# A mixture-of-experts kernel whose expert rows move through device memory, with wider weight blocks and one stream of weight tiles

## The reference, cut to what matters

```python
D_MODEL, N_EXPERTS, TOP_K = 1024, 8, 2
D_FF = 2816

def swiglu(x, wg, wu, wd):
    return jnp.dot(jax.nn.silu(jnp.dot(x, wg)) * jnp.dot(x, wu), wd)

def moe_swiglu(x, router, wg, wu, wd):        # all in float32
    xf = x.reshape(-1, shp[-1])
    logits = jnp.dot(xf, router).astype(jnp.float32)
    top_v, top_i = lax.top_k(logits, TOP_K)
    probs = jax.nn.softmax(top_v, axis=-1)
    gate = jnp.sum(jax.nn.one_hot(top_i, N_EXPERTS, dtype=jnp.float32) * probs[..., None], axis=1)
    y = jnp.zeros(xf.shape, jnp.float32)
    for e in range(N_EXPERTS):
        y = y + gate[:, e:e + 1] * swiglu(xf, wg[e], wu[e], wd[e]).astype(jnp.float32)
    return y
...
x = layer_norm(DEEPNORM_ALPHA * x + moe_swiglu(...), ln_ffn_g[1], ln_ffn_b[1])
```

## Time and profile before

| what | value |
|---|---|
| time, median of 3 runs | 1351.56 us (1350.29 to 1352.23) |
| span of the profiled execution, first to last instruction | 1350.1 us |
| profiled execution's own time | not listed apart; its span is 0.2 to 2.1 us under the three times |
| PE busy | 1262.2 us, 93% |
| DVE busy / ACT busy / POOL busy | 1046.8 / 802.5 / 56.5 us |
| DMA moved | 332.66 MB, mean 246 GB/s |
| mean granted TensorE clock | 0.974 |

### The profile page before, as it was taken

One profiled execution on the slowest core, in us unless ns is written; L12 is line 12 of the kernel. 1 busy time (PEld: TensorE's weight loads), 2 busy tenths in 40 slices (PEclk: granted clock), 3 DMA queues, 4 the chain that ended last, 5 costly groups with the idle time before them and its releaser, 6 DMA issues.

```text
span 1350.1 us, 22286 instructions
## 1 busy us (share of the span) xinstructions
PE 1262.2 (93%) x8696; PEld 1174.4 (87%) x8696; DVE 1046.8 (78%) x1016; ACT 802.5 (59%) x901; POOL 56.5 (4%) x34
## 2 busy tenths in 40 slices
PE   6999999989875989999999999999999999999993
PEld 4899999979874869999998998998998998998992
DVE  6734343469998668889889889888888888888886
ACT  3533333354653456766776766776776776776771
POOL 0000000001642000000000000000000000000000
PEclk9999999999887989999999999999999999999997
DMA  9854444253030407998998998998998998998931
GB/s 276 266 172 157 159 158 150 60 158 105 13 121 32 156 32 237 370 358 284 370 361 277 367 363 278 366 363 275 367 363 279 366 350 292 365 366 282 366 140 37
DMA packets 249538, 332.66 MB, mean 246 GB/s; under 512 B 6404, under 2 KB 222820, under 8 KB 249450
## 3 DMA queue, kind: packets, MB, share of 16 engines
q1 hardware_dynamic: 249283, 331.28, 73.2%
q10 hardware_dynamic: 199, 0.62, 0.2%
HBM read 330.44 MB, written 2.84 MB: 247 GB/s over the span
## 4 chain that ended last, share of the span: by engine, by line
PE 80%; DVE 14%; ACT 3%; issue 2%; DMA 1%; DVEq 0%; ACTq 0%
PE bank L1068 35%; PE bank L1088 18%; PE bank L889 15%; PE bank L918 6%; DVE cacc L1321 5%; PE bank L1032 2%; PE bank L1077 1%; PE bank L838 1%; DVE w_lo L1165 1%; PE bank L1053 1%; ACT w_hi L543 1%; DVE acc L1469 1%; DMA spool<-in_state_pool_dram 1%; PE bank L874 1%; DVE uc_lo L1349 1%
## 5 line engine op out<-in xcount | busy, mean ns | idle before, releaser
L1165 DVE TENSOR_TENSOR w_lo<-raw,w_hi 128x2048 fp32r<-128x2048 f32 x309 | 707.9, 2292 | 200.7 <-ACT w_hi L543 200.1
L543 ACT CAST w_hi<-raw 128x2048 fp32r<-128x2048 f32 x309 | 590.9, 1913 | 260.2 <-PE bank L889 107.6
L1068 PE MATMUL bank<-w_hi,xg_hi 128*128 128x256 f32 x1408 | 401.6, 285 | 5.3 <-DVE acc L1469 3.6
L1068 PE MATMUL bank<-w_hi,xg_lo 128*128 128x256 f32 x1408 | 394.0, 280 | 0.0
L1068 PE MATMUL bank<-w_lo,xg_hi 128*128 128x256 f32 x1408 | 393.9, 280 | 0.0
L1068 PEld LDWEIGHTS bank<-w_hi,xg_hi 128*128 128x128 f32 x1408 | 265.4, 189 | 13.2 <-issue 8.9
L1068 PEld LDWEIGHTS bank<-w_lo,xg_hi 128*128 128x128 f32 x1408 | 266.0, 189 | 3.2
L1068 PEld LDWEIGHTS bank<-w_hi,xg_lo 128*128 128x128 f32 x1408 | 265.2, 188 | 0.0
L889 PE MATMUL bank<-x_hi,w_hi 128*128 128x304 f32 (+1 forms) x544 | 166.2, 305 | 8.5 <-DVE x_lo L1252 5.3
L889 PE MATMUL bank<-x_hi,w_lo 128*128 128x304 f32 (+1 forms) x544 | 164.3, 302 | 0.0
L889 PE MATMUL bank<-x_lo,w_hi 128*128 128x304 f32 (+1 forms) x544 | 163.6, 301 | 0.0
(11 more groups left out here) (191 smaller groups left out, 1337.8 us busy)
## 6 DMA issues: line engine op xcount, KB each, us to landing
raw<-in_moe_w_gate_dram SPq DMA_DIRECT2D x88, 1024.0 KB, 5.6
raw<-in_moe_w_up_dram SPq DMA_DIRECT2D x88, 1024.0 KB, 5.9
raw<-in_moe_w_down_dram SPq DMA_DIRECT2D x88, 1024.0 KB, 5.2
raw<-in_conv_w_dram SPq DMA_DIRECT2D x12, 1024.0 KB, 5.4
raw<-in_ffn_w_gate_dram SPq DMA_DIRECT2D x11, 1024.0 KB, 8.0
raw<-in_ffn_w_up_dram SPq DMA_DIRECT2D x11, 1024.0 KB, 8.1
raw<-in_ffn_w_down_dram SPq DMA_DIRECT2D x11, 1024.0 KB, 4.9
poolw<-in_pool_w_dram SPq DMA_DIRECT2D x1, 1024.0 KB, 11.1
```

Source lines behind the costliest of these rows:

```text
L543: act.copy(w_hi[t % SPLIT][:], raw[t % RAW][:]).then_inc(hi_ready, 1)
L1068: last = pe.matmul(bank[:, 0:TW], x[:, c, :], w[:, c, :], start=(c == 0 and k == 0), stop=(c == KC - 1 and k == 2))
L1165: dve.tensor_tensor(w_lo[t % SPLIT][:], raw[t % RAW][:], w_hi[t % SPLIT][:], ALU.subtract).then_inc(split_ready, 1)
```

## The change

Rows are no longer picked and spread by matmuls. The kernel makes a table `x_dram` in device memory (8 experts x 384 rows of 4 KB) and fills it with zeros from SBUF during the dense gate and up phase: 24 transfers of 0.5 MB on SP's queue, and one for the first 128 rows of `y_dram`. After the router, POOL writes each of the 288 rows to the places of its two experts by 6 indirect DMAs, the offsets `row_i` coming from a few small DVE steps. ACT's queue loads an expert's 128 rows as `xg_rows`, an expert ahead; PE transposes them as before. Each of the first seven experts' outputs is copied to `y_rows` by ACT and stored to `y_dram`. During the last expert POOL fetches each row's two outputs (6 indirect DMAs into freed ring buffers), and DVE adds them to `acc` with weights `w_a` and `w_b` in 6 steps of 128 x 1024. Only the last expert still goes through `sel`, `sel_t` and the 12 scatter matmuls.

Gate and up blocks are 512 columns wide, two tiles each (512 of the 1024 rows, rows of 2 KB); a tile is 12 matmuls of 512 columns. 2816 columns are five such blocks and one of 256. There are still 33 tiles an expert. Their order is g g u u d d, the down tiles being those of the block before. The stream runs on over experts: the next expert's first gate and up tiles stand before the last down tile of this one.

The core of the diff:

```diff
+    BW = 2 * TW
+    NB = (F + BW - 1) // BW
+    def body_tiles(last):
+        tiles = []
+        for j in range(1, NB):
+            for kind in "gu":
+                tiles += [(kind, j, half) for half in range(width(j) // TW)]
+            tiles += [("d", j - 1, half) for half in range(width(j - 1) // TW)]
+        if not last:
+            tiles += [("next " + kind, 0, half) for kind in "gu" for half in range(width(0) // TW)]
+        return tiles + [("d", NB - 1, half) for half in range(width(NB - 1) // TW)]
...
+                if i >= 4 and EMPTY_ROWS // 6 * (i - 4) < EMPTY_ROWS:
+                    for k in range(EMPTY_ROWS // 6 * (i - 4), EMPTY_ROWS // 6 * (i - 3)):
+                        sp.dma_start(x_dram[k * P:(k + 1) * P, :], zero_rows[:]).then_inc(empty, 16)
...
+            pool.wait_ge(empty, 16 * EMPTY_ROWS)
+            pool.wait_ge(rows_known, 1)
+            for i in range(3):
+                pool.wait_ge(x_rows_done, 2 * i + 2)
+                for k in range(2):
+                    pool.indirect_dma_start(x_dram[:, :], bass.IndirectOffsetOnAxis(ap=row_i[0:n, i, k:k + 1], axis=0),
+                                            acc[0:n, i, :], None).then_inc(x_scattered, 16)
+            def one_pass(r):
+                pool.wait_ge(pair_ready, r + 1)
+                pool.wait_ge(split_ready, r * (E * TE) + SPARE_FREE)
+                pool.wait_ge(y_stored, (r + 1) * (16 * (E - 1)) + 16)
+                for k in range(2):
+                    for i in range(3):
+                        pool.indirect_dma_start(y_got[k][i][0:n, :], None, y_dram[:, :],
+                                                bass.IndirectOffsetOnAxis(ap=pair_i[0:n, k, i:i + 1], axis=0))\
+                            .then_inc(y_fetched, 16)
...
+            def load_rows(r, e):
+                act.dma_start(xg_rows[:], x_dram[bass.ds(e * ROWS + r * P, P), :]).then_inc(xg_landed, 16)
...
             def one_expert(r, e, last):                                   # ACT
+                if not last:
+                    load_rows(r, e + 1)
+                for k, (kind, j, half) in enumerate(LAST if last else BODY):
+                    if k + SPLIT < len(tiles) or not last:
+                        hi(t + SPLIT, n)
+                    if kind == "g" and half == width(j) // TW - 1:
+                        turn_evac(n, j - 1)
+                        silu(n, j, t)
...
+                    act.wait_ge(y_stored, (r * (E - 1) + e) * 16 + 16)
+                    for k in range(2):
+                        act.copy(y_rows[:, k * HALF:(k + 1) * HALF], ps[6 + k][:, :]).then_inc(y_out, 1)
+                    act.wait_ge(y_out, 2 * n + 4)
+                    act.dma_start(y_dram[bass.ds(e * P, P), :], y_rows[:]).then_inc(y_stored, 16)
...
+            act.wait_ge(x_scattered, 16 * 6)
+            load_rows(0, 0)
...
-            def gather_rows(g):                                           # PE
...
+            def turn_rows(g):
+                pe.wait_ge(xg_landed, 16 * g + 16)
...
+            def rows_block(n, t, bank, j, half):
+                wh, wl = block_of(w_hi[t % SPLIT], j), block_of(w_lo[t % SPLIT], j)
+                chunks = range(4 * half, 4 * half + 4) if width(j) == 2 * TW else range(KC)
+                for c in chunks:
+                    for k, (x, w) in enumerate(((xg_hi, wh), (xg_hi, wl), (xg_lo, wh))):
+                        last = pe.matmul(bank[:, 0:width(j)], x[:, c, :], w[:, c - chunks[0], :],
+                                         start=(c == 0 and k == 0), stop=(c == KC - 1 and k == 2))
...
+            def add_fetched(r, k, i):                                     # DVE
+                dve.scalar_tensor_tensor(out=acc[0:n, i, :], in0=y_got[k][i][0:n, :], scalar=(w_a, w_b)[k][0:n, i:i + 1],
+                                         in1=acc[0:n, i, :], op0=ALU.mult, op1=ALU.add).then_inc(y_added, 1)
```

More of the change, by code:

```diff
@@ L785, in one_pass @@
+            def one_pass(r):
+                n = r * E
+                xg_evac(n)
+                for p, (kind, j, half) in enumerate(LEAD):
+                    hi(T_MOE + p + SPLIT, n)
+                    if kind == "g" and half == width(0) // TW - 1:
+                        silu(n, 0, T_MOE + p)
                 with act.Fori(0, E - 1) as e:
@@ new lines, in turn_h, with down @@
+            def turn_h(n, j):
+                pe.wait_ge(h_done, n * NB + (FC + j + 1))
+                for s in range(width(j) // P):
+                    last = pe.transpose(ps[4 + j % 2][:, s * P:(s + 1) * P], hn[:, s * P:(s + 1) * P], ident[:])
+                last.then_inc(h_turned, 1)
+            def down(n, t, j, half):
+                pe.wait_ge(split_ready, n * TE + (t + 1))
+                pe.wait_ge(ht_lo_done, n * NB + (j + 1))
+                if j == 0 and half == 0:
+                    pe.wait_ge(y_out, 2 * n + 2)
+                wh, wl = tall(w_hi[t % SPLIT]), tall(w_lo[t % SPLIT])
+                for s in range(TR):
+                    for col in range(2):
+                        cols = slice(col * HALF, (col + 1) * HALF)
+                        for k, (x, w) in enumerate(((ht_hi, wh), (ht_hi, wl), (ht_lo, wh))):
+                            last = pe.matmul(ps[6 + col][:, :], x[:, 2 * half + s, :], w[:, s, cols],
+                                             start=(j == 0 and half == 0 and s == 0 and k == 0),
+                                             stop=(j == NB - 1 and s == TR - 1 and k == 2))
+                last.then_inc(tile_used, 1)
@@ L1457, in _ @@
[L1457 to L1471 removed]
+            one, two = row_of[:, :, 0], row_of[:, :, 1]
@@ new lines, in _ @@
+            (base_a, base_b, slot_a, slot_b, left_a, left_b, gate_a, gate_b, first, other, below, in_a, in_b, at_a,
+             at_b, far_b, w_a, w_b) = (pair[:, i, :] for i in range(18))
+            dve.tensor_tensor(first, one, two, ALU.is_lt)
+            dve.tensor_tensor(other, one, two, ALU.is_gt)
+            dve.tensor_tensor(base_a, top_f[:, :, 0], top_f[:, :, 1], ALU.min)
+            dve.tensor_tensor(base_b, top_f[:, :, 0], top_f[:, :, 1], ALU.max)
+            dve.tensor_tensor(slot_a, one, two, ALU.min)
@@ new lines, in _ @@
+            link(dve.tensor_tensor(slot_b, one, two, ALU.max))
+            dve.tensor_tensor(gate_a, first, prob[:, :, 2], ALU.mult)
+            dve.tensor_tensor(at_a, other, prob[:, :, 3], ALU.mult)
+            dve.tensor_tensor(gate_b, other, prob[:, :, 2], ALU.mult)
+            dve.tensor_tensor(at_b, first, prob[:, :, 3], ALU.mult)
+            dve.tensor_scalar(below, base_b, float(E - 1), None, ALU.is_lt)
+            dve.scalar_tensor_tensor(out=left_a, in0=base_a, scalar=-float(ROWS), in1=slot_a, op0=ALU.mult, op1=ALU.add)
@@ L1473, in xg_low, with select @@
+            def select(e):
+                for i in range(3):
+                    last = dve.tensor_scalar(sel[:, i, :], slot_no[:], slot_of[:, i, e:e + 1], None, ALU.is_equal)
+                last.then_inc(sel_ready, 1)
             def xg_low(g):
```

593 lines of the change are left out of this document (296 added, 297 removed).

## The result

The changed kernel takes 1319.63 us (median of four runs, 1316.71 to 1320.77) against 1350.92 (1349.76 to 1352.23): a ratio of 0.9764, 95% interval 0.975 to 0.9777. The forecast was 1302 with a range of 1292 to 1322; the point is 18 us too low. The profiled execution took 1320.68 us with a span of 1318.8.

The account below looks back on a forecast made before the run. PE was taken to bound the kernel, with DMA near its limit. Span 1350.1, less 62.5 for the stream, plus 10.4 at the start and 2.1 at the end, gave 1300.1, so 1301.6 us (likeliest 1302), range 1292 to 1322.

Parts of the forecast that it names:

- B: Rival at expert borders: ACT's issues or the store's wait cost 2.5 us a border, not 0.5; 1316 us, chance 0.11.
- C: Rival at the start: indirect scatter DMAs take 4.45 us each, start at 530; 1319 us, chance 0.12.
- A: The forecast's own mechanism for the whole kernel: likeliest 1302 us, own range 1293 to 1309, chance 0.66.
- five signs of being right: Expert period near 94.7 us, wide tile 2.75, PE's only DMA wait the first, first weight matmul near 513, end 27.
- A wide tile takes 2.75 us: Expert stream on PE: 12 matmuls of 512 columns cost a down tile's 2.75 us, bounds 2.56 and 2.83.
- At least 1 us is left everywhere: Inside an expert: ACT's and DVE's copies, splits and ht_lo are ready at least 1 us before PE wants them.
- 0.5 us of stall at a border: Between experts: ACT's crowded queue costs nothing to 2 us a border; 0.5 taken, 3.5 for seven.
- DMA: Expert stream: DMA stays just behind PE, 93.4 us an expert against PE's 94.7, needing 364 GB/s.
- D: Rival in the stream: DMA paces it, all bytes held to 348 GB/s; stream 793, time 1335 us, chance 0.04.
- E: Rival in the stream: two DMA queues together drag the rate, slower than before if below 341 GB/s; chance 0.04.
- The start: Router to first weight matmul: six scatters 12 us, row load, transposes and split; 513.1, 10.4 later than before.
- F: Rival: 512 columns bring nothing and new stalls lose half the saving; 1326 us or more, chance 0.03.

Follow-up runs that it names:

- e9: e1 with its small SBUF buffers, stationary operands among them, at the bytes they had in the kernel before, including a 64-byte pad; 1297.8 us, ratio 0.9615.
- e12: e1 with only a pad of 64 bytes, moving every buffer behind the constants and keeping their order; 1299.53 us, ratio 0.962.
- e1: Changed kernel, but at an expert's narrow block ACT evacuates ht_hi and DVE makes ht_lo before the next tile's split; 1307.48 us, ratio 0.9679.
- e4: Changed kernel, but in the mixture DVE computes only the first quarter of each w_lo tile; single run, 1307.9 us.
- e3: Changed kernel, but each expert tile's load moves only 64 KB of its 1 MB; single run, 1315.67 us.
- e7: e1 with each wide tile loaded as 1024 rows of 1 KB instead of 512 of 2 KB; 1307.99 us, ratio 0.9685.
- e5: Changed kernel with blocks of 256 columns and every evacuation, row transposes' too, ahead of the next split; 1327.68 us, ratio 0.9835.
- e11: e1 with ScalarE making only the first quarter of each expert w_hi and VectorE of each w_lo; single run, 1307.45 us.
- e10: e1 plus 54 small filler matmuls while PE waits for the first expert's rows; 1307.52 us, ratio 0.9686.

## Why the forecast was right, and where it was not

The mechanism held in the main: the removed gather, scatter and `sel` work leaves the stream, the ring keeps up, and the start pays part of it back. That the time lies inside the range is in part luck. The forecast gave its own mechanism 1293 to 1309, and 1319.6 is outside of that. The range reached to 1322 to take in B and most of C, and neither came; two terms of A itself were wrong instead, by as much. Of the five signs of being right three came; the expert's period of 94.7 us and the wide tile of 2.75 did not (97.0 and 2.80). By its steps:

- **A wide tile takes 2.75 us**: the term that failed first. It measured 2.80 in the changed kernel. The form was right: e9 and e12 have 2.75. What I did not look at is that the diff moves the matmuls' stationary operands. `xg_hi` begins at byte 207680 of a partition before, 64 past a multiple of 128; after at 187136, a multiple of 128; in e12 at 187200, 64 past it again. `w_hi` and `w_lo` begin at multiples of 128 in all of them. The narrow matmuls show the same, 118.8 ns against 117.0 before and in e9 (117.4 in e12). Price: 10.5 us, shown by undoing it. The pad moves every buffer behind the constants. That the stationary operands are the ones that count is argued: of the moved buffers a weight matmul reads no other. It is not shown, nor is why, and no start but 0 and 64 was tried.
- **"At least 1 us is left everywhere"**: failed at the one narrow block of an expert, which my schedule did not place. Its up tile covers 2.85 us; the split of the next tile (2.29) stands in DVE's queue ahead of `ht_lo` (0.69). Price: 10.9 us over the stream, shown by e1 and, another way, by e4; 1.8 of it is the lower clock behind the last wait.
- **0.5 us of stall at a border**: 3.5 in the sum. With order and place mended the stream is 758.0 to 758.1 against 759.6; if the other terms hold, some 2 us of stall remain. B's 2.5 a border did not come: an expert takes the 94.7 of the forecast in e9 and e12, so ACT's copies and issues are nearly hidden. Six weight loads wait 3.0 us in all for `w_lo` in e12.
- **DMA**: right. No wait of `w_hi` for `raw` in the mixture, and 94% fewer bytes change nothing (e3), nor do shorter rows (e7). That excludes D and E. A single core takes 384 to 392 GB/s in the page's best slices. The Trainium skill (DMA: Bandwidth & Descriptors, Specifications) gives about 358 as a core's HBM limit, a stack's bandwidth shared by two cores. A single core runs here and this trace is above it, as was the one before.
- **The start**: 12 us for the six scatters measured 10.1 (505.64 - 495.56), the load 3.3 for 3.6, transposes and split 3.3 for 3.4; the indices came 1.4 later than forecast. Together 512.32 for 513.1. The 12 was a choice between wide bounds, so that it came so near is luck in part. The lower figure that the prediction gives, 7.4, counts a fixed 2.0 us once for all six transfers; the trace has 10.1. C's 4.45 us each is excluded by the 1.26.
- **The end**: 27.0 for 27.4. **The zeros**: no price in the dense phase, as costed; `w_hi` waits for `raw` once there, 0.7 us, and 1.2 before.

The two failed terms are 21.4 us of stream; the measured miss is 19.9, since the other terms, the border stalls among them, were costed 1.5 too dear. F's premise, that 512 columns bring nothing, was true of the changed kernel by accident: six tiles 17.24 us against 17.26. With the operands in their place they bring 17.26 - 16.94 = 0.32 us for six tiles, 14 us over 44 such periods.

The prediction reads the slices a little too smoothly: the mixture's full rates begin with the seventeenth slice, not the sixteenth (237), and one of the later ones is 350. Nothing rests on it.

## What to carry to other kernels

When a change alters anything ahead of a packed SBUF layout, compare the start addresses of the matmuls' operands modulo 128 before comparing times; a pad of 64 bytes was worth 0.6% here. In a schedule by hand, place the odd block (the narrow, the last, the first) by itself: a copy on which PE waits belongs ahead of a split that can be late, above all where a single tile is the cover. A wait of 2 us on a busy PE can cost nearly as much again in clock. And cost the parts by where they lie. With blocks of 256 columns the row travel gains 23 us over the kernel before (e5 against its 1350.4); blocks of 512 gain 20 more (e1), of which only 8 are shorter tiles and most of the rest stalls and sums that they avoid (both with their operands at a multiple of 128); the longer DMA rows gain nothing (e7).

## What the runs showed of the hardware

- Where the packed buffers begin, the stationary operands among them, changes the matmul's step: 229.1 ns at 64 past a multiple of 128 bytes (e9, e12), 232.8 at a multiple (after, e1), for 512 columns with a weight load each, at full clock. With most of the work of DMA, VectorE or ScalarE beside it taken away it is 232.7 to 233.1 (e3, e4, e11). The Trainium skill (SBUF — State Buffer, Operand start alignment) asks only for a start at a multiple of the element size and says that its measurements are about legality, not speed; both places satisfy it, and the runs here time the difference.
- A wait can cost the clock as well. Behind 2.07 us of idle PE the granted clock was 0.50 and a down tile took 4.59 us for 2.80 (after, last expert); behind 2.3 us a down tile took 4.61 for 2.79 (e5). Behind seven waits of 0.8 us it stayed at 1.00.
- Six indirect DMAs of up to 128 rows of 4 KB follow each other at 1.26 us on POOL's queue, and the last has landed 2.7 us after it begins there (3.8 in e10).
- A filler matmul of 128 columns in plain fp32 leaves two records of 0.12 us; with a chain of them the granted clock is 0.81 from 496 to 500 us and 1.00 (2.4 GHz) from there on, where e1's waiting PE has 0.50 (1.2 GHz) from 500 to 512.
